# The order of states, levels and forget projection inside an HGRN head of a hybrid decoder step

## What is computed

```python
# q, f, i, g: projections of the normed input, 128 wide per head
log_f = log(lb + (1 - lb) * sigmoid(f));  k = (1 - lb) * sigmoid(-f);  q = silu(q)
# per token t, state S (128 x 128):
S_t = diag(f_t) S_{t-1} + k_t v_t^T
o_t = S_t^T q_t
out = rmsnorm(o) * hg_norm * silu(g)
# in chunks: b = cumsum(log_f) inside a chunk
att[t, s] = sum_k q[t, k] k[s, k] exp(b[t, k] - b[s, k])   for s <= t
o = att v + (q exp(b)) S_before
S = diag(exp(b_last)) S_before + (k exp(b_last - b))^T v
```

## Time and profile before

| | |
|---|---|
| median of 3 runs | 3127.73 us |
| lowest and highest | 3123.15 and 3129.18 us |
| profiled execution, its own time | 3130.01 us |
| its span, first to last instruction | 3128.2 us |
| mean granted TensorE clock | 0.943 |
| TensorE matmuls busy | 2876.7 us (92%) |
| VectorE busy | 1367.4 us (44%) |
| ScalarE busy | 1325.0 us (42%) |
| one HGRN head, 635.9 to 677.6 us: TensorE, VectorE, ScalarE busy | 37.01, 32.89, 23.23 of 41.70 us |

### The profile page before, as it was taken

The page is one execution under the profiler, slowest core; times in us unless marked ns, Lnnn a source line. Parts: engine busy times, 40 slices in busy tenths (PEclk is TensorE's granted clock), DMA queues, the critical chain, the costliest instruction groups (busy, mean ns, idle before and its releaser), DMA issues.

```text
span 3128.2 us, 58782 instructions
## 1 busy us (share of the span) xinstructions
PE 2876.7 (92%) x23719; PEld 2434.2 (78%) x23719; DVE 1367.4 (44%) x2587; ACT 1325.0 (42%) x1798; POOL 40.5 (1%) x74
## 2 busy tenths in 40 slices
PE   5999996989799979899998999998988989899996
PEld 3899876778688868699887899876856557789996
DVE  2444327778555553544324444331124343444433
ACT  2555335555222234555434554332123334455542
POOL 0000000000000000000000000000000000000000
PEclk7999998999889979999998999998999998999998
DMA  6223441221121214222342223431255524322221
GB/s 233 81 94 119 174 152 62 75 82 69 64 71 70 104 60 186 74 96 98 144 175 79 94 94 124 175 113 69 108 165 157 170 94 177 128 81 94 99 95 62
DMA packets 58187, 348.90 MB, mean 112 GB/s; under 512 B 7474, under 2 KB 7811, under 8 KB 28515
## 3 DMA queue, kind: packets, MB, share of 16 engines
q1 hardware_dynamic: 52274, 322.85, 29.2%
q0 software_dynamic: 5808, 24.59, 2.2%
HBM read 334.96 MB, written 12.45 MB: 111 GB/s over the span
## 4 chain that ended last, share of the span: by engine, by line
PE 84%; DVE 7%; ACT 4%; DVEq 2%; issue 2%; DMA 1%; ACTq 0%; SPq 0%; POOL 0%
PE PS L816 54%; PE PS L781 10%; PE PS L830 2%; PE PS L798 2%; PE PS L1212 1%; PE PS L854 1%; PE PS L1194 1%; PE PS L1197 1%; PE PS L1173 1%; PE PS L949 1%; PE PS L838 1%; DMA weight_ring<-in_ada_w 1%; PE PS L1204 1%; DVE arena L2108 1%; DVE sub_out L1780 1%
## 5 line engine op out<-in xcount | busy, mean ns | idle before, releaser
L1725 DVE TENSOR_TENSOR w_rest<-weight_ring,w_hi 128x1024 bf16<-128x1024 f32 (+1 forms) x304 | 363.5, 1196 | 870.8 <-ACT w_hi L1376 866.6
L1376 ACT ACTIVATE w_hi<-weight_ring 128x1024 fp32r<-128x1024 f32 (+1 forms) x304 | 315.3, 1037 | 853.2 <-PE PS L816 844.6
L816 PE MATMUL PS<-hid_hi,w_hi 128*128 128x260 f32 x2688 | 363.4, 288 | 2.1 <-ACT w_hi L1376 2.1
L816 PEld LDWEIGHTS PS<-hid_hi,w_hi 128*128 128x128 f32 x2688 | 332.6, 188 | 5.5 <-issue 3.2
L816 PE MATMUL PS<-hid_rest,w_bf 128*128 128x260 bf16 x2688 | 329.7, 274 | 0.0
L816 PE MATMUL PS<-hid_bf,w_rest 128*128 128x260 bf16 x2688 | 327.8, 274 | 0.0
L1377 ACT ACTIVATE w_bf<-weight_ring 128x1024 bf16<-128x1024 f32 (+1 forms) x304 | 309.1, 1017 | 0.0
L816 PEld LDWEIGHTS PS<-hid_bf,w_rest 128*128 128x128 bf16 x2688 | 260.4, 97 | 40.3
L816 PEld LDWEIGHTS PS<-hid_rest,w_bf 128*128 128x128 bf16 x2688 | 247.2, 97 | 43.3
L781 PE MATMUL PS<-hidden,weight_ring 128*128 128x260 f32 x896 | 205.0, 392 | 12.9 <-ACTq L525 8.9
L781 PEld LDWEIGHTS PS<-hidden,weight_ring 128*128 128x128 f32 x896 | 174.7, 196 | 41.9 <-ACTq L525 9.3
(11 more groups left out here) (403 smaller groups left out, 4075.2 us busy)
## 6 DMA issues: line engine op xcount, KB each, us to landing
weight_ring<-in_ffn_gu SPq DMA_DIRECT2D x88, 1024.0 KB, 4.8
ada_chunks<-in_ada_w SPq DMA_DIRECT2D x40, 1536.0 KB, 6.5
weight_ring<-in_ffn_wd SPq DMA_DIRECT2D x32, 1408.0 KB, 6.0
weight_ring<-in_w_hgrn SPq DMA_DIRECT2D x16, 1024.0 KB, 4.9
weight_ring<-in_ada_w SPq DMA_DIRECT2D x8, 1536.0 KB, 7.9
weight_ring<-in_w_ssm SPq DMA_DIRECT2D x8, 1536.0 KB, 6.5
weight_ring<-in_mla_pairs SPq DMA_DIRECT2D x8, 1536.0 KB, 6.6
weight_ring<-in_w_out_ab SPq DMA_DIRECT2D x8, 1024.0 KB, 8.3
```

Source lines behind the costliest of these rows:

```text
L816: last = pe.matmul(PS[:, bank + hf, 0:HT], w[:, buf, k * P:(k + 1) * P], x[:, first + k, hf * HT:(hf + 1) * HT], start=start and w is w_hi ...
L1376: act.activation(hi[:, buf, 0:n], src, ACT.Copy).then_inc(w_hi_ready, 1)
L1725: tt(WL_[:, buf, 0:n], W[:, slot, j * DC * P:j * DC * P + n], WH[:, buf, 0:n].bitcast(F32), ALU.subtract).then_inc(w_rest_ready, 1)
```

## The change

On TensorE the state products, and behind them the FORGET projection of the next head, stand in front of the loop of eight steps; before, the state products stood behind step 0 and FORGET behind the loop. The sample outputs, with their wait for `s_new`, stand in front of the attention outputs, with their three waits. On ScalarE the KDT copy stands between the FORGET and the QUERY cut instead of behind both. On VectorE the sample states and the chunk states stand behind the FORGET cut, in front of the QUERY cut and of the copies of the eight steps; before, they stood behind those copies. No instruction is added or removed.

```diff
@@ -973,6 +973,12 @@
                     for c in range(NCH):
                         last = pe.transpose(PS[:, 4, c * P:(c + 1) * P], KD[:, c * CH:(c + 1) * CH], IDENT)
                     last.then_inc(h_kt, 1)
+                    pe.wait_ge(h_kdt, h + 1)
+                    for c in range(NCH):
+                        last = pe.matmul(PS[:, 5, c * P:(c + 1) * P], KDT[:, c, :], VV[:, c, :], start=True, stop=True)
+                    last.then_inc(h_u, 1)
+                    if more:
+                        project(h + 1, FORGET, 2)
                     for n in range(1 + len(LEVELS)):
 
                         if n >= 1:
@@ -988,14 +994,11 @@
                                 last = pe.matmul(PS[at:at + m, n % 2, col:col + m], lhs[:, keys:keys + m],
                                                  rhs[:, queries:queries + m], start=True, stop=True)
                         last.then_inc(h_p, 1)
-                        if n == 0:
-                            pe.wait_ge(h_kdt, h + 1)
-                            for c in range(NCH):
-                                last = pe.matmul(PS[:, 5, c * P:(c + 1) * P], KDT[:, c, :], VV[:, c, :],
-                                                 start=True, stop=True)
-                            last.then_inc(h_u, 1)
-                    if more:
-                        project(h + 1, FORGET, 2)
+                    pe.wait_ge(s_new, h + 1)
+                    for b in range(NB):
+                        last = pe.matmul(PS[:, 7, b:b + 1], S0[:, b, :], QS[:, NP_ + b:NP_ + b + 1],
+                                         start=True, stop=True)
+                    last.then_inc(h_o, 1)
                     pe.wait_ge(h_vk, h + 1)
                     pe.wait_ge(h_att, h + 1)
                     pe.wait_ge(h_s, h + 1)
@@ -1004,11 +1007,6 @@
                         last = pe.matmul(PS[:, 6, cc], VV[:, c, :], AT[:, c, :], start=True, stop=(c == 0))
                         if c:
                             last = pe.matmul(PS[:, 6, cc], ST[:, c - 1, :], QI[:, cc], start=False, stop=True)
-                    last.then_inc(h_o, 1)
-                    pe.wait_ge(s_new, h + 1)
-                    for b in range(NB):
-                        last = pe.matmul(PS[:, 7, b:b + 1], S0[:, b, :], QS[:, NP_ + b:NP_ + b + 1],
-                                         start=True, stop=True)
                     last.then_inc(h_o, 1)
 
                     def sums():
@@ -1463,9 +1461,10 @@
                     act.activation(VS, PS[0:NB, 7, 0:P], ACT.Copy).then_inc(h_v, 1)
                     if more:
                         cut(h, FORGET, 1)
-                        cut(h, QUERY, 1)
                     act.wait_ge(h_kt, h + 1)
                     act.activation(KDT.rearrange("p a b -> p (a b)"), PS[:, 4, :], ACT.Copy).then_inc(h_kdt, 1)
+                    if more:
+                        cut(h, QUERY, 1)
                     if more:
                         both_tables()
                         forget_exp(h, 1)
@@ -1905,6 +1904,24 @@
                         tt(d[:, :, 0, :], d[:, :, 0, :], k[:, :, 0, :], ALU.mult).then_inc(h_qk, 1)
                     if more:
                         cut(h, FORGET, 1)
+                    dve.wait_ge(s_loaded, h * 16 + 16)
+                    dve.wait_ge(h_vb, h + 1)
+                    tt(S0, S0, bcast(FG[:, NP_:T], 2, P), ALU.mult)
+                    for b in range(2):
+                        tt(VK[:, 4 * b:4 * b + 4, :], PS[:, 6 + b, :].rearrange("p (a b) -> p a b", a=4),
+                           bcast(KK[:, NP_ + 4 * b:NP_ + 4 * b + 4], 2, P), ALU.mult)
+                    dve.drain().then_inc(h_vk, 1)
+                    tt(S0, S0, VK, ALU.add).then_inc(s_new, 1)
+
+                    dve.wait_ge(h_u, h + 1)
+                    dve.wait_ge(s_stored, h + 1)
+                    dve.tensor_copy(ST[:, 0, :], PS[:, 5, 0:P])
+                    for c in range(1, NCH):
+                        dve.drain()
+                        stt(ST[:, c, :], ST[:, c - 1, :], EB[:, (c + 1) * CH - 1:(c + 1) * CH],
+                            PS[:, 5, c * P:(c + 1) * P], ALU.mult, ALU.add)
+                    dve.drain().then_inc(h_s, 1)
+                    if more:
                         cut(h, QUERY, 1)
 
                     for n in range(1 + len(LEVELS)):
@@ -1928,23 +1945,6 @@
                         dve.tensor_copy(AT[at:at + QR_, :, at:at + QR_], AB[at:at + QR_])
                     dve.drain().then_inc(h_att, 1)
 
-                    dve.wait_ge(s_loaded, h * 16 + 16)
-                    dve.wait_ge(h_vb, h + 1)
-                    tt(S0, S0, bcast(FG[:, NP_:T], 2, P), ALU.mult)
-                    for b in range(2):
-                        tt(VK[:, 4 * b:4 * b + 4, :], PS[:, 6 + b, :].rearrange("p (a b) -> p a b", a=4),
-                           bcast(KK[:, NP_ + 4 * b:NP_ + 4 * b + 4], 2, P), ALU.mult)
-                    dve.drain().then_inc(h_vk, 1)
-                    tt(S0, S0, VK, ALU.add).then_inc(s_new, 1)
-
-                    dve.wait_ge(h_u, h + 1)
-                    dve.wait_ge(s_stored, h + 1)
-                    dve.tensor_copy(ST[:, 0, :], PS[:, 5, 0:P])
-                    for c in range(1, NCH):
-                        dve.drain()
-                        stt(ST[:, c, :], ST[:, c - 1, :], EB[:, (c + 1) * CH - 1:(c + 1) * CH],
-                            PS[:, 5, c * P:(c + 1) * P], ALU.mult, ALU.add)
-                    dve.drain().then_inc(h_s, 1)
                     if more:
                         forget(h, 1)
 
```

## The result

The change made the kernel slower: 3136.93 us (median of 6 runs, 3125.95 to 3139.22) against 3128.42 us (6 runs, 3123.15 to 3131.78), a ratio of 1.0028 with a 95% interval of 1.0017 to 1.0038. Timed again beside the first experiments it was 3135.0 us against 3126.37, ratio 1.0035 (1.0021 to 1.0048). Predicted were 3122 us and a range of 3115 to 3131.

A forecast was written before the change was run, and what follows sets the result against it. TensorE carries 84% of the chain of waits, but in the HGRN heads TensorE's queue and VectorE's chain both bound. Seven heads -2.5 us and last head -3.5 give -6.0, from 3127.7 to 3122.0 us; range 3115 to 3131.

The forecast's parts named there:

- the clock decides the size: HGRN heads: one half-clock stretch per head slows FORGET; -0.7 us for five heads, +0.5 for two, -2.5 in all.
- Rival B: Half-clock stretch keeps its length, over FORGET: +0.5 to +1.0 us per head, last head -3.5; 3129.5 us; chance 0.23.
- Rival C: A second half-clock stretch per head, slowing attention outputs and QUERY: 1.75 us per head at 6.8 us; 3134 us; chance 0.14.
- part 4: Sample outputs ahead of attention outputs: TensorE's path 9.8 to 8.1 us, VectorE's longer by 1.65; no gain alone.
- The slower side: Outcome with a second half-clock stretch: 12.3 us over seven heads, with -6.0 gives +6.3 us, 3134; chance 0.14.
- A: Main forecast: low stretch mostly short over FORGET, seven heads -2.5 us, last head -3.5; 3116 to 3126 us; chance 0.50.
- The first head: First HGRN head, counted among the seven with a next head, at -0.7 or +0.5 us like the others.
- Part 3: FORGET ahead of levels (5.53 us) against states ahead of level copies (5.46): nearly even swap; forget gate -1.24 us at full clock.
- The last head: Last HGRN head, without FORGET or cuts: squares start earlier by 2.7 to 6.1 us, taken as -3.5 us.
- the products 0.69 us behind the transposes: KDT copied ahead of the QUERY cut: state products at 653.83 in place of 654.79, -0.96 us in the fourth head.
- VectorE's 9.8 us path from forget gate to GATE: VectorE from forget gate to the next GATE: stays 9.76 us and becomes the longer path by 1.65 us.
- S0, the stores and the weight loads at no cost: Queues: states stored earlier, S0's load covered by 13 us, QUERY's weight slot freed 5.5 us later; no cost.

The follow-up runs named there:

- the split kernel: Changed kernel with attention outputs ahead of the sample outputs and FORGET's third pass held back behind the levels; 3122.26 us against 3125.74 for the kernel before, ratio 0.9987.

## Why the prediction was wrong

**The step that failed is "the clock decides the size".** I took a stretch of 3.4 us, with 0.53 us lost over FORGET, for five heads of seven. In the six loop steps of the first trace it was 3.4 us once, 6.8 three times and 10.2 twice, and from its first matmul to level 0 FORGET took 6.4 to 7.7 us instead of 5.7, a loss of 0.7 to 2.0 us. The price for each length was about right: for 3.4 us -0.7 was written and -0.7 came at the forget gate; for 6.8 us +0.5 to +1.0 was written and +0.5 came. The lengths were wrong, and 10.2 us, at +2.1, was not among them. Rival B, with a chance of 0.23, had this mechanism, but with stretches at most as long as before.

**Rival C's stretch came as well**, in all these heads, 3.4 to 6.8 us long. At 3.4 us it cost nothing in the six steps, as part 4 said, since VectorE's path was the longer; at 6.8 us, in two steps of six in either trace, it cost 1.1 us where 1.75 was written. The cause that I gave is not borne out: without the swap of outputs the stretch came too, and the levels use the same two banks in turn in the split kernel, where no fall followed them in the loop. Part of the evidence against C was misread. The earlier trace rows show one low stretch of the last head before, but that head has two more, and one of them lies over its attention outputs, behind the levels and a wait of 7.1 us (TensorE's row of the windows view):

```profile
830.90:837.70 6.80, 3.55 (x17) 0.50 0.21 86
```

The slower side came out right in sign and time (3134 predicted, 3137 and 3135 measured). With the terms it was made of, that is partly luck: it had seven prices of 1.75 for C's stretch and A's gain for FORGET, where the runs show a loss over FORGET, 1.1 us in a third of the steps, and the first head.

**The first head was priced like the others.** The seven heads of the sum are those with a next one, so the first, ahead of the first close, is among them at -0.7 or +0.5. It lost 3.9 and 3.7 us, of sums of +5.3 and +7.6: in the first trace 2.9 ahead of its forget gate, 1.0 behind it. I had read no row of it. It had a stretch of 10.2 us before the change already:

```profile
523.70:533.90 10.20, 9.69 (x116) 0.50 0.28 94
```

**Part 3's -1.24 us was no gain of the order.** It compared level copies at full clock (5.74 us) with the same at half (6.52), and an early KDT copy with a late one: 0.78 and 0.96 us, more than the whole. The old order gets both as well when it has the full clock and the dense matmuls in front of the copy: 40.9 us against 41.1.

**The last head** was predicted at -3.5 us; it gave -5.7, -1.7 and, alone, -6.5. The bounds I wrote, 2.7 to 6.1, were too narrow on both ends.

**Right were**: the products 0.69 us behind the transposes; VectorE's states done before level 0 can come; VectorE's 9.8 us path from forget gate to GATE and its 1.65 us lead, seen as 1.80 at full clock; S0, the stores and the weight loads at no cost. That the two moves of part 3 are nearly an even swap was right as well; the term for the clock then had the wrong sign.

Open: why a given head gets the short or the long stretches, and what starts the second one. The steps of 42.1 and 43.8 us stand side by side in one trace.

## What to carry to other kernels

Here thin work was the place where a half clock cost least, since VectorE set its pace: levels and copies took 6.52 us instead of 5.74, while FORGET took up to 7.7 instead of 5.7. Before dense matmuls are moved to stand behind selections and short waits, read from the windows view which stretch of the head has the low clock and ask what will lie in it afterwards; splitting the dense work, so that a pass of it separates the thin parts, was worth 27 us here between two kernels that differ in nothing else. And in a cycle in which two engines' paths are equally long, shortening one alone gives nothing, while the slack that a move leaves on one of them can be what absorbs the next disturbance.

## What the runs showed of the hardware

The clock fell with TensorE busy nearly all the time. Ahead of the second stretch of the fifth head (from 717.4) the last 3.4 us were full of small matmuls:

```profile
713.90:717.30 3.40, 3.29 (x81) 1.00 0.00 0
```

It also fell behind waits, in the last head of the kernel before after 7.1 us of idle time. The first stretch of a head begins around the selections, whose stationary operand has 8 of 128 rows; the longest waits near them are 0.83 and 0.69 us. That the 8 rows are the cause is not shown, since no run changed them alone. Seventeen dense matmuls among them kept the clock at 1.00 in five steps of one kernel and four of another, and then not in the next, with the same instructions. Two executions of the same program differed by 4 us in one head (35.1 and 39.1) with the mean clock at 0.83 and 0.69.

The Trainium skill, "TensorE: Matmul & The Clock Gate", Part 1, has the low clock as the default that activity lifts. The trace agrees in that the stretch from 697.0 ended within FORGET, 4.4 us behind its first matmul; it doesn't show why the clock fell at 717.4, behind 3.29 of 3.40 us of matmuls.
